# Attention scores kept in their PSUM banks for the maximum and the exponential, the mask's edge added by TensorE, and conditioning products placed between the turned heads

## What is computed

```python
def sink_softmax(s, sink):
    m = jnp.maximum(jnp.max(s, axis=-1, keepdims=True), sk)
    p = jnp.exp(s - m)
    return p / (jnp.sum(p, axis=-1, keepdims=True) + jnp.exp(sk - m))
...
        valid = (kpos[None, :] >= 0) & (kpos[None, :] < T) & (jnp.abs(qpos[:, None] - kpos[None, :]) <= WINDOW)
        s_win = jnp.einsum('bqkgd,bskd->bkgqs', qblk, kw).astype(jnp.float32) * scale
        s_win = jnp.where(valid[None, None, None], s_win, NEG)
        s_ctx = jnp.einsum('bqkgd,bskd->bkgqs', qblk, k_ctx).astype(jnp.float32) * scale
        p = sink_softmax(jnp.concatenate([s_win, s_ctx], axis=-1), sink).astype(v.dtype)
        return (jnp.einsum('bkgqs,bskd->bqkgd', p[..., :span], vw)
                + jnp.einsum('bkgqs,bskd->bqkgd', p[..., span:], v_ctx))
```

## Time and profile before

| | us |
|---|---|
| median of 3 runs | 780.11 |
| lowest, highest run | 777.83, 780.56 |
| the profiled execution: its own time | 780.54 |
| the profiled execution: span from the first to the last instruction | 778.7 |

### The profile page before, as it was taken

One profiled execution on the slowest core, in us unless ns is written; L12 is line 12 of the kernel. 1 busy time (PEld: TensorE's weight loads), 2 busy tenths in 40 slices (PEclk: granted clock), 3 DMA queues, 4 the chain that ended last, 5 costly groups with the idle time before them and its releaser, 6 DMA issues.

```text
span 778.7 us, 9993 instructions
## 1 busy us (share of the span) xinstructions
PE 757.7 (97%) x3907; PEld 373.9 (48%) x3907; DVE 381.4 (49%) x820; ACT 173.8 (22%) x431; POOL 2.4 (0%) x12
## 2 busy tenths in 40 slices
PE   8999997999999999999999999999999999999997
PEld 3364545445544345344435758445545344344334
DVE  2216196126742544445327996726742543445326
ACT  4111565016221101110114301116221101110111
POOL 0000000000000000000000000000000000000000
PEclk9999999999999999999999999999999999999999
DMA  8979999125899999999999986155599999999995
GB/s 342 429 234 431 427 430 425 67 108 218 324 385 424 427 425 425 428 430 428 422 416 424 427 362 254 70 216 215 214 378 421 428 427 425 426 431 428 422 416 201
DMA packets 32851, 277.04 MB, mean 356 GB/s; under 512 B 7790, under 2 KB 8834, under 8 KB 12834
## 3 DMA queue, kind: packets, MB, share of 16 engines
q1 hardware_dynamic: 32305, 274.96, 85.6%
q10 hardware_dynamic: 432, 1.28, 0.4%
q0 software_dynamic: 64, 0.13, 0.0%
HBM read 274.65 MB, written 1.70 MB: 355 GB/s over the span
## 4 chain that ended last, share of the span: by engine, by line
PE 87%; DVE 6%; ACT 2%; issue 1%; DVEq 1%; DMA 1%; SPq 0%; ACTq 0%
PE bank L2136 29%; PE bank L2161 14%; PE bank L2002 11%; PE bank L2167 5%; PE bank L2115 5%; PE bank L2561 5%; PE bank L2431 4%; PE bank L2392 3%; PE bank L1930 2%; DMA ring<-in_ada_w 1%; DVEq L1328 1%; PE bank L2147 1%; PE bank L2142 1%; PE bank L2555 1%; ACT T L1077 1%
## 5 line engine op out<-in xcount | busy, mean ns | idle before, releaser
L2136 PE MATMUL bank<-ring,Z 128*64 128x512 f32 x1024 | 226.5, 594 | 0.0
L2136 PEld LDWEIGHTS bank<-ring,Z 128*64 128x64 f32 x1024 | 71.8, 137 | 137.5 <-issue 135.4
L2161 PE MATMUL bank<-ring,Z 128*64 128x512 f32 (+1 forms) x544 | 113.9, 570 | 0.0
L2002 PE MATMUL bank<-ring,T 128*128 128x512 f32 x192 | 83.6, 593 | 0.4 <-issue 0.4
L2161 PEld LDWEIGHTS bank<-ring,Z 128*64 128x64 f32 x544 | 37.5, 137 | 68.4 <-issue 66.3
L1606 DVE TENSOR_TENSOR Z<-Z,bank 128x512 f32<-128x512 f32 x16 | 11.0, 688 | 119.4 <-PE bank L2136 119.4
L2002 PEld LDWEIGHTS bank<-ring,T 128*128 128x128 f32 x192 | 36.0, 190 | 44.6 <-issue 44.6
L2167 PE MATMUL bank<-ys,Cs 128*128 128x512 f32 (+1 forms) x204 | 52.1, 390 | 1.1 <-DVE ys L1623 1.1
L1600 DVE COPY Z<-bank 128x512 f32<-128x512 f32 x24 | 16.6, 692 | 73.7 <-PE bank L2115 73.7
L1636 DVE TENSOR_TENSOR x<-x,bank 128x512 f32<-128x512 f32 x84 | 51.9, 682 | 0.3
L1214 ACT ACTIVATE ys<-wg 128x512 fp32r<-128x512 f32 (+1 forms) x34 | 20.6, 605 | 131.2 <-DVE wg L1618 131.2
(11 more groups left out here) (256 smaller groups left out, 776.5 us busy)
## 6 DMA issues: line engine op xcount, KB each, us to landing
ring<-in_moe_w SPq DMA_DIRECT2D x62, 2048.0 KB, 15.4
ring<-in_moe_w SPq DMA_DIRECT2D x60, 1024.0 KB, 10.7
ring<-in_ada_w SPq DMA_DIRECT2D x23, 2048.0 KB, 18.1
ring<-in_moe_w SPq DMA_DIRECT2D x16, 512.0 KB, 19.5
ring<-in_a_w_out SPq DMA_DIRECT2D x2, 2048.0 KB, 14.9
ring<-in_f_w_in SPq DMA_DIRECT2D x2, 2048.0 KB, 26.0
ring<-in_f_w_out SPq DMA_DIRECT2D x2, 2048.0 KB, 20.1
ring<-in_ada_w SPq DMA_DIRECT2D x2, 1024.0 KB, 8.6
```

Source lines behind the costliest of these rows:

```text
L2002: last = pe.matmul(b[:, :], T[:, k, i * P:(i + 1) * P], w[:, k, :], start=(k == 0), stop=(k == KT - 1))
L2136: last = pe.matmul(out[BLK * u:BLK * (u + 1), :], xT[:, b, k, s0 + BLK * u:s0 + BLK * (u + 1)], w[:, k, :], start=(k == 0), stop=(k == KT ...
L2161: last = pe.matmul(out, aT[:, k, BLK * u:BLK * (u + 1)], down_columns(w2, k, a, e), start=(k == 0), stop=(k == FC - 1), skip_group_check=True)
```

## The change

The scores are no longer copied to SBUF. VectorE's `maxima` reads each bank for the maximum only (L1811 of the changed kernel), and the scale is applied to the four maxima. ScalarE's exponential reads the bank itself, with the scale in the instruction (L1128), writes to SBUF as before, and now is what empties the bank. The mask is added by TensorE: after the four score products of a latent group come four small products in bf16, an identity with the 128 x 128 block of the mask that is not zero (L2488), accumulated on the banks. Two bf16 tiles, `ident_bf` and `edges_bf`, are made on VectorE ahead of the rotary step.

The scores get the banks 0 to 3 (head n the bank n % 4). The turned heads and the transposed conditioning rows take turns on the banks 4 and 5. The products `ada_product` 9 to 13 move from between the groups to between the second and third turned head of a group. On ScalarE one more group of exponentials stands ahead of the copies of turned heads, and VectorE's `normalize(2, 1)` stands ahead of `ada_read(13)`.

```diff
+    out["edges"] = np.concatenate([mask[0:P, P:], mask[P:, 0:P]], 1)
+    out["room"] = np.zeros((P, 4 * P))
...
+    t.banks = list(range(4, JOINED_BANK))
+
     def scores(i, half):
         for n in range(4 * half, 4 * half + 4):
-            t.add(("score", i, n), "dve")
...
+            t.add(("score", i, n), "act", bank=n % 4)
+
+    def values(i, half, block=None):
         for n in range(4 * half, 4 * half + 4):
+            if n == 4 * half + 2 and block is not None:
+                ada_product(block)
             t.add(("PT", i, n), "act")
...
                 for n in range(4):
+                    b = stage_bank(("score", i, 4 * half + n), act)
                     pr = heads(i, 4 * half + n, 4 * half + n + 1)[:, 0, 0:w]
-                    act.activation(pr, pr, ACT.Exp, bias=nmx[:, n:n + 1], accum_out=den[:, n:n + 1])
+                    emptied_inc(act.activation(pr, b[:, 0:w], ACT.Exp, scale=HD ** -0.5, bias=nmx[:, n:n + 1],
+                                               accum_out=den[:, n:n + 1]))
...
             exps(0, 0)
             exps(0, 1)
-            ada_product(9)
-            turned(0, 0)
             exps(1, 0)
+            turned(0, 0, 9)
+            exps(1, 1)
             turned(0, 1)
-            exps(1, 1)
+            exps(2, 0)
             turned(1, 0)
-            exps(2, 0)
+            exps(2, 1)
             turned(1, 1)
-            exps(2, 1)
-            ada_product(13)
-            turned(2, 0)
+            turned(2, 0, 13)
             turned(2, 1)
...
+            def maxima(i, half):
...
+                mx, nmx, den, es = stats(i, half)
                 for n in range(a, e):
...
+                    bank, filled = turn[("score", i, n)][0:2]
+                    dve.wait_ge(full, filled)
+                    dve.tensor_reduce(mx[:, n - a:n - a + 1], banks[bank][:, 0:w], AX.X, ALU.max)
+                settle()
+                dve.scalar_tensor_tensor(mx, mx, HD ** -0.5, sink[:, a:e], ALU.mult, ALU.max)
                 settle()
                 dve.tensor_scalar(nmx, mx, -1.0, None, ALU.mult)
                 dve.tensor_tensor(es, sink[:, a:e], mx, ALU.subtract).then_inc(p_max, 1)
...
+                for n in range(4 * half, 4 * half + 4):
+                    if i > 0:
+                        other = slice((2 - i) * P, (3 - i) * P)
+                        pe.matmul(banks[turn[("score", i, n)][0]][:, other], ident_bf[:, :], edges_bf[:, i - 1, :],
+                                  start=False, stop=True, skip_group_check=True).then_inc(full, 1)
```

More of the change, by code:

```diff
@@ L139, in attention_columns @@
     q, k = tok[:, None], tok[None, :]
-    mask = np.where(np.abs(q - k) <= WINDOW, 0.0, -1e30)
-    mask = np.concatenate([mask, np.zeros((DEC, PAST))], 1)
-    out["mask"] = mask.reshape(2, P, DEC + PAST).transpose(1, 0, 2).reshape(P, -1)
+    mask = np.where(np.abs(q - k) <= WINDOW, 0.0, -2.0 ** 100)
+    assert not mask[0:P, 0:P].any() and not mask[P:, P:].any()
+    out["edges"] = np.concatenate([mask[0:P, P:], mask[P:, 0:P]], 1)
+    out["room"] = np.zeros((P, 4 * P))
     def band(T, w):
@@ L407, in plan @@
         t.add(("qT", c), "act")
+    t.banks = list(range(4, JOINED_BANK))
     def scores(i, half):
         for n in range(4 * half, 4 * half + 4):
-            t.add(("score", i, n), "dve")
-    def values(i, half):
+            t.add(("score", i, n), "act", bank=n % 4)
+    def values(i, half, block=None):
         for n in range(4 * half, 4 * half + 4):
+            if n == 4 * half + 2 and block is not None:
+                ada_product(block)
             t.add(("PT", i, n), "act")
@@ L423, in plan @@
     scores(1, 0)
-    ada_product(9)
-    values(0, 0)
+    values(0, 0, 9)
     scores(1, 1)
     ada_read(9)
-    ada_product(10)
-    values(0, 1)
+    values(0, 1, 10)
     scores(2, 0)
-    ada_product(11)
-    values(1, 0)
+    values(1, 0, 11)
     scores(2, 1)
-    ada_product(12)
-    values(1, 1)
-    ada_product(13)
-    values(2, 0)
+    values(1, 1, 12)
+    values(2, 0, 13)
     ada_read(13)
@@ L647, in build @@
         zone(D - HIGH_SPLIT)
+        room_at = ATT["room"][0]
+        ident_bf = sb_over("ident_bf", [P, P], BF16, "special", room_at)
+        edges_bf = sb_over("edges_bf", [P, 2, P], BF16, "special", room_at + P // 2)
         S1 = special[:, 0:NT * QUAD].rearrange("p (t s) -> p t s", t=NT)
@@ L1117, in exps, with turned @@
                 mx, nmx, den, es = stats(i, half)
+                if (i, half) == (1, 0):
+                    act.wait_ge(kv_out_done, 32)
                 for n in range(4):
+                    b = stage_bank(("score", i, 4 * half + n), act)
                     pr = heads(i, 4 * half + n, 4 * half + n + 1)[:, 0, 0:w]
-                    act.activation(pr, pr, ACT.Exp, bias=nmx[:, n:n + 1], accum_out=den[:, n:n + 1])
+                    emptied_inc(act.activation(pr, b[:, 0:w], ACT.Exp, scale=HD ** -0.5, bias=nmx[:, n:n + 1],
+                                               accum_out=den[:, n:n + 1]))
                 act.activation(es, es, ACT.Exp).then_inc(p_exp, 1)
-            def turned(i, half):
+            def turned(i, half, block=None):
                 w = SEQ if i == 0 else TOK
                 for n in range(4 * half, 4 * half + 4):
+                    if n == 4 * half + 2 and block is not None:
+                        ada_product(block)
                     b = stage_bank(("PT", i, n), act)
@@ L1774, in _ @@
             dve.wait_ge(special_in, 16)
+            dve.tensor_copy(ident_bf[:, :], ident)
+            dve.tensor_copy(edges_bf.rearrange("p i n -> p (i n)"), att("edges"))
             for i in (1, 2):
@@ L1791, in _ @@
             gate_parts(5)
-            def scores(i, half):
+            def maxima(i, half):
                 w = SEQ if i == 0 else TOK
                 a, e = 4 * half, 4 * half + 4
+                mx, nmx, den, es = stats(i, half)
                 for n in range(a, e):
[L1797 to L1803, removed]
-                settle()
[L1805 to L1812, removed]
+                    bank, filled = turn[("score", i, n)][0:2]
+                    dve.wait_ge(full, filled)
+                    dve.tensor_reduce(mx[:, n - a:n - a + 1], banks[bank][:, 0:w], AX.X, ALU.max)
+                settle()
+                dve.scalar_tensor_tensor(mx, mx, HD ** -0.5, sink[:, a:e], ALU.mult, ALU.max)
                 settle()
@@ L1832, in attended @@
                 emptied_inc(dve.tensor_copy(T[:, 0:4, i * P:(i + 1) * P], b[:, :].rearrange("p (c n) -> p c n", c=4)))
-            scores(0, 0)
-            scores(0, 1)
+            maxima(0, 0)
+            maxima(0, 1)
             normalize(0, 0)
-            dve.wait_ge(kv_out_done, 32)
-            scores(1, 0)
+            maxima(1, 0)
             normalize(0, 1)
-            scores(1, 1)
+            maxima(1, 1)
             ada_read(9)
@@ L1844, in _ @@
             attended(0)
-            scores(2, 0)
+            maxima(2, 0)
             normalize(1, 1)
-            scores(2, 1)
+            maxima(2, 1)
             normalize(2, 0)
             attended(1)
+            normalize(2, 1)
             ada_read(13)
-            normalize(2, 1)
             attended(2)
@@ L2482, in scores, with values @@
                     keys = kT[rows_, 0:SEQ] if i == 0 else kT[rows_, SEQ:TOK + PAST]
-                    pe.matmul(b[:, 0:keys.shape[1]], q, keys, start=True, stop=True).then_inc(full, 1)
-            def values(i, half):
+                    last = pe.matmul(b[:, 0:keys.shape[1]], q, keys, start=True, stop=(i == 0), skip_group_check=True)
+                    if i == 0:
+                        last.then_inc(full, 1)
+                for n in range(4 * half, 4 * half + 4):
[3 more added lines that the diff above has]
+                                  start=False, stop=True, skip_group_check=True).then_inc(full, 1)
+            def values(i, half, block=None):
                 pe.wait_ge(p_ready, 2 * i + half + 1)
@@ L2509, in values @@
                 for n in range(a, a + 4):
+                    if n == a + 2 and block is not None:
+                        ada_product(block)
                     turn_head(n)
```

## The result

The changed kernel is slower: 794.24 us (median of 4 runs, 793.49 to 796.38) against 779.95 us before. The ratio on record is 1.0193, 95% interval 1.0164 to 1.0221 (the quotient of the two medians, 1.0183, lies inside it). The forecast was 798, with a range from 789 to 805.

What follows compares the result with a forecast made beforehand. TensorE, busy for 97% of the span, was taken to bound the kernel. The profiled 780.5 us + 11.2 for a longer attention stage + 6.8 for the clock gave 798.5, forecast as 798 us, range 789 to 805.

Steps and rivals of the forecast that it cites:

- the reading of row 9: Round of (1, 1): second short head also waits for VectorE's read behind the maxima; scores of (2, 0) 9.8 us late.
- the banks of (0, 0): Stage start: scores of (0, 1) wait for the exponentials to free them, done at 99.4; scores of (1, 0) 3.0 us late.
- all of it its own work: Attention stage before the change: TensorE needs 5.2 to 6.6 us between groups' scores, with no waiting in it.
- The walk: Step-by-step pass through the attention stage against the earlier starts; it claimed the stage ends 11.2 us later.
- The rounds: From one group's scores to the next: maxima, exponentials, copy, heads and products follow on one another, 9.7 us when full.
- The clock: Attention stage: TensorE's granted clock falls after waits of about 3 us, costing 6.8 us in all (0 to 11.6).
- the four waits: About 3 us each, before third heads of (0, 0), (1, 0), (1, 1) and second of (0, 1); 1.7 us of clock each.
- the second rival: Attention stage: the clock stays full because TensorE works two thirds of each round; 791 us, chance 0.17.
- The transfers: Weight loads: no limit, the projection's second block landing by 117 us, long before the stage ends.
- It falls at every wait: Attention stage: the clock drops at each wait and stays low over the scores too; 803 us, chance 0.17.
- The faster rival: Attention stage: TensorE's own work sets the length, both large waits and the half clock go, masks come; 775 us, chance 0.06.

Runs made afterwards that it cites:

- the order alone: Kernel before the change, with only ScalarE's exponentials of the next group moved ahead of the copies of turned heads: 800.33 us, ratio 1.0259.
- copies first: Changed kernel with ScalarE's copies of a group's turned heads put back ahead of the next group's exponentials: 787.20 us, ratio to before 1.0097.
- the products ahead: Changed kernel with conditioning products 9 to 13 put back between the groups, ahead of the first turned head: 796.56 us.
- VectorE's order alone: Kernel before the change, with only VectorE's normalization of (2, 1) moved ahead of reading conditioning row 13: 775.51 us, ratio 0.9956.
- the banks alone: Kernel before the change, with only scores in banks 0 to 3, turned heads and transposed conditioning rows in 4 and 5: 783.57 us, ratio 1.0051.
- product 7 moved: Changed kernel with conditioning product 7 moved between the scores of (0, 0) and those of (0, 1): 793.61 us.

## Why the prediction was right

**The mechanism** is as forecast, place by place. The third heads of (0, 0), (1, 0) and (1, 1) wait 2.8 to 3.0 us for ScalarE's copy, the second head of (0, 1) 2.07 for the reading of row 9, ScalarE 4.7 to 7.6 us for the maxima. Two experiments show it from both sides: undoing the order takes 7.0 us away, and the order alone adds 20.9 to the kernel before. The forecast also named the two places that hold the other half, the banks of (0, 0) and the reading of row 9. It read TensorE's rounds of before as "all of it its own work"; they hold waits of 0.53 and 0.21 us for copies, which is small beside the loss.

**The walk.** The banks for the scores of (0, 0) were to come free at 95.3 and 95.7, and the scores started at 95.26. Those of (0, 1) were to be done at 99.4 and were at 99.7. Those of (1, 0) came at 105.56 instead of 103.0: 2.4 of it the two products behind the first fall of the clock, the rest the scores ahead of them, which it slowed too. The rounds were 9.0, 8.7 and 9.7 in the forecast and 8.3, 8.4 and 9.5 in the trace. The single prices: four maxima 2.0 and 1.95; four masks 0.4 and 0.23 (107.06 to 107.29); exponentials up to the first copy 2.5 and 2.33 (109.86 to 112.19). The last two terms are a little too large. The first copy took 0.55 us with 384 columns, as forecast (128.90 to 129.45), and 0.34 with 128, where the walk had 0.55 too. The stage end came 13.5 late; less 3.8 for the clock (below) this is 9.7 against 11.2 forecast.

**The clock** is the term that was mis-sized: "I take 1.7 for each: 6.8 us". There were two falls, and only one of them at one of the four waits. The first cost 2.4 us in the conditioning products (6.00 less 3.64), the second 1.4: the six transposes at 138.95 took 1.54 us against 0.93 at 129.45, and the products up to their end 0.8 more than those at 130.32. Together 3.8. The step also had the place wrong: the first fall was at the start of the stage, at waits that the walk had (0.93 and 1.70) and did not price; three waits of 2.99, 2.07 and 2.78 us brought none. The same start cost less in two other traces: the two products took 5.34 us with copies first and 4.68 with the products ahead. The four executions of the changed kernel lie between 793.5 and 796.4, and the slowest has a mean clock of 0.989 where the others have 0.993, so the time at the lower clock differs from run to run.

**The two add up.** 1.5 too much in the walk and 3.0 in the clock are the 4.5 us between 18.0 forecast and 13.5 for the stage. In the median, 14.3 us. The forecast's 798 is 3.8 us too high, and the 791 of the second rival, "the clock holds", is 3.2 too low, so the median by itself does not choose between them; the two falls in the trace do, for the first. There is some luck in it: 2.4 of the 3.8 us for the clock came from a place that the forecast priced at nothing, and of the 6.8 for the four waits 1.4 came.

**The transfers** stayed out of it, as forecast: a share of 0.00 from 153.2 to 173.9 us, and the length behind the stage is the same.

**The rivals.** "It falls at every wait", 803, is what the order alone did on the kernel before (800.3, waits of 3.4 us or more), and what the changed kernel did with the products ahead of the heads (796.6, waits of 2.1 to 3.3 us). In the second the falls cost less than the 2.9 us each that 803 supposes. The Trainium skill's rule of the oscillation (TensorE: Matmul & The Clock Gate, section "HAM oscillation — how this bites in real kernels"), by which short bursts with waits between them have the clock lowered again at each wait, agrees with those two runs and not with the changed kernel, where three of four such waits brought no fall. The faster rival's 775 is near the 775.5 that VectorE's order alone gives, but by another sum: that run keeps the wait of 1.00 us and adds no masks.

## What to carry to other kernels

- A queue that runs in order makes a bank's release depend on everything ahead of it. Before moving the emptying of a bank to another engine, write down what stands ahead of it there; here one place in ScalarE's program was worth 7 us in one kernel and 21 in the other (5 of them by the clock), and the deal of the banks 4 in the kernel before.
- Work taken from an engine gains only where that engine's step ends a wait. The 1.7 us a group taken from VectorE brought no gain over the kernel before in any run; it can have helped only where the new order had put the maxima on the path, and there it is part of the 6 us between the changed kernel and the order alone. Moving one VectorE step that nobody was waiting for behind one that TensorE was waiting for was worth 3.8 us with no work removed.
- When several edits arrive together, try each small one alone: the part worth keeping was the smallest.

## What the hardware did that I had not expected

- Waits of about the same length differ in what the clock does. In the changed kernel 2.99, 2.07 and 2.78 us brought no fall and 2.77 did; 0.93 and 1.70 with small score products between them did. A wait of 2.91 us ahead of the same heads brought a fall in the profile of the kernel before and with the order alone, and none with the banks alone. With the order alone, waits of 3.4 to 4.9 us each brought one.
- Whether a conditioning product in the middle of the heads protects the clock is supported but not shown: two falls against five with the product ahead, and mean clocks of 0.989 to 0.993 against 0.989 to 0.991 over four executions each. Against it stands the run with product 7 moved, where the product was in the middle and the wait of 3.00 us brought a fall.
- In these traces the exponential from a PSUM bank is slightly quicker than from SBUF: one in 0.57 us from start to start against 0.61 (109.86 to 110.43, and 105.40 to 106.01 before), its sum included.
- A bf16 mask of 128 columns cost TensorE 0.06 us of its path (0.23 for four), under half the 0.13 of an fp32 transpose of that size.
